# Second block's attention: probabilities turned one step later, evictions in steps of their own, bias tables issued by SyncE

## The reference, cut to what matters

```python
s = jnp.einsum('bhrnqd,bhrnkd->bhrnqk', qb, kb) * (HEAD_DIM ** -0.5)
s = s - slopes * dist            # dilated heads; masked, softmax, times v
...
s = jnp.where(mask, s + bias[None], NEG_INF)   # neighbourhood heads
p = jax.nn.softmax(s, axis=(-2, -1))
o = jnp.einsum('bhijqckl,bhijkld->bhijqcd', p, vg)
...
y_dil = rms_norm(y_dil, g_out_dil); y_na = rms_norm(y_na, g_out_na)
h = h + jnp.concatenate([y_dil, y_na], axis=-1) @ w_out
```

## Time and profile before

| | us |
|---|---|
| median of 3 runs | 2672.23 |
| lowest and highest of them | 2665.27, 2678.31 |
| the profiled execution's own time | 2675.64 |
| its span, first to last instruction | 2673.8 |
| TensorE busy over the span | 2409.8 (90%) |
| VectorE busy | 1320.0 (49%) |
| ScalarE busy | 1060.9 (40%) |
| GpSimd busy | 655.6 (25%) |

### The profile page before, as it was taken

One profiled execution on the slowest core, in us unless ns is written; L12 is line 12 of the kernel. 1 busy time (PEld: TensorE's weight loads), 2 busy tenths in 40 slices (PEclk: granted clock), 3 DMA queues, 4 the chain that ended last, 5 costly groups with the idle time before them and its releaser, 6 DMA issues.

```text
span 2673.8 us, 31894 instructions
## 1 busy us (share of the span) xinstructions
PE 2409.8 (90%) x12186; PEld 1879.8 (70%) x12186; DVE 1320.0 (49%) x2106; ACT 1060.9 (40%) x1619; POOL 655.6 (25%) x293
## 2 busy tenths in 40 slices
PE   4998977979999999979987889999989998959998
PEld 2875734858888788857564567888868765647776
DVE  3436943144341244225386215525433377539998
ACT  4324621243332233225264035434332355327776
POOL 1220000142222222232200043444454400112223
PEclk8998968979999999979998889999999988979999
DMA  6530041113322232213302232323323211229997
GB/s 229 180 103 6 1 157 48 32 32 103 111 64 64 88 107 75 63 40 117 103 6 111 79 126 72 102 87 102 102 63 110 87 49 35 95 106 341 345 350 267
DMA packets 81032, 291.17 MB, mean 109 GB/s; under 512 B 10713, under 2 KB 13050, under 8 KB 79932
## 3 DMA queue, kind: packets, MB, share of 16 engines
q1 hardware_dynamic: 71952, 251.26, 27.5%
q10 hardware_dynamic: 6348, 28.51, 3.1%
q0 software_dynamic: 2592, 9.48, 0.9%
HBM read 283.43 MB, written 9.48 MB: 110 GB/s over the span
## 4 chain that ended last, share of the span: by engine, by line
PE 75%; DVE 13%; ACT 3%; DMA 2%; issue 2%; POOL 2%; DVEq 2%; SPq 0%; ACTq 0%; POOLq 0%
PE ps L598 36%; PE ps L645 11%; PE ps L621 4%; DVE mlo L2369 4%; PE ps L1221 3%; PE ps L706 2%; DVE stat L1949 2%; PE ps L1239 2%; DVE ptl L1965 2%; PE ps L1093 2%; PE ps L1048 2%; DVE pr L1957 1%; PE ps L946 1%; POOL x L547 1%; PE ps L1066 1%
## 5 line engine op out<-in xcount | busy, mean ns | idle before, releaser
L541 POOL TENSOR_TENSOR wlo<-wraw,whi 128x1024 fp32r<-128x1024 f32 x208 | 502.3, 2416 | 1581.1 <-ACT whi L1261 936.5
L598 PE MATMUL ps<-hhi,whi 128*128 128x512 f32 x1624 | 590.3, 363 | 3.0 <-DVE hlo L2071 2.0
L598 PE MATMUL ps<-hlo,whi 128*128 128x512 f32 x1624 | 584.1, 360 | 0.0
L598 PE MATMUL ps<-hhi,wlo 128*128 128x512 f32 x1624 | 581.1, 358 | 0.0
L598 PEld LDWEIGHTS ps<-hhi,whi 128*128 128x128 f32 x1624 | 306.7, 189 | 72.3 <-issue 19.6
L598 PEld LDWEIGHTS ps<-hhi,wlo 128*128 128x128 f32 x1624 | 305.7, 188 | 47.9
L598 PEld LDWEIGHTS ps<-hlo,whi 128*128 128x128 f32 x1624 | 306.5, 189 | 45.3 <-issue 1.0
L1824 DVE SCALAR_TENSOR_TENSOR up<-ps,cconv,up 128x511 f32<-128x511 f32 (+1 forms) x132 | 83.2, 658 | 292.6 <-ACT up L1570 290.1
L2369 DVE TENSOR_TENSOR mlo<-mraw,mhi 128x1024 fp32r<-128x1024 f32 x147 | 206.5, 1434 | 6.9 <-ACT mhi L1693 6.8
L1268 ACT ACTIVATE whi<-wraw 128x1024 fp32r<-128x1024 f32 x132 | 138.9, 1052 | 149.9 <-PE ps L645 120.3
L645 PE MATMUL ps<-alo,whi 128*128 128x512 f32 (+1 forms) x528 | 188.0, 356 | 0.0
(11 more groups left out here) (337 smaller groups left out, 4248.7 us busy)
## 6 DMA issues: line engine op xcount, KB each, us to landing
wraw<-in_w_all SPq DMA_DIRECT2D x288, 512.0 KB, 3.5
mraw<-in_w_moe SPq DMA_DIRECT2D x168, 512.0 KB, 5.4
mraw_b<-in_w_mod SPq DMA_DIRECT2D x10, 512.0 KB, 15.5
fl<-in_four ACTq DMA_DIRECT2D x2, 2048.0 KB, 8.1
hd<-in_hyf ACTq DMA_DIRECT2D x2, 2048.0 KB, 8.3
hi<-in_hyi ACTq DMA_DIRECT2D x2, 2048.0 KB, 13.4
slot_rows<-in_slot_rows ACTq DMA_DIRECT2D x1, 3612.0 KB, 20.9
xs<-slot_rows POOLq DMA_DIRECT2D x7, 516.0 KB, 7.0
```

Of the source, the lines that this page charges most:

```text
L541: pool.tensor_tensor(wlo[:, slot, :], wraw[:, AT_W[n] % RING, :], whi[:, slot, :].bitcast(F32), ALU.subtract).then_inc(lo_split, 1)
L598: m = pe.matmul(ps[:, bank + b, 0:w], a, r[:, c0:c0 + w], start=k == 0 and q == 0, stop=k == KT - 1 and q == 2)
```

## The change

- The transposes of step i take the probabilities of step i-3 (T_LAG = 3) instead of i-2, and the outputs are 7 steps behind (O_LAG) instead of 6.
- ScalarE, in a step: high half of the turned probabilities of step i-3 first, then the exponential of i. The exponential's own wait for the transposes goes, since the first has it.
- The values are evicted in steps 0, 8, 16, ... by ScalarE and in steps 1, 9, ... by VectorE (before: 0, 6, 14, ... on both). TensorE still turns them in 0, 6, 14, ....
- The outputs are evicted in steps 14, 22, ..., the squares in 15, 23, ..., the outputs' low halves in 16, 24, ... (before: 13, 13, 14 and every 8 behind).
- The table's subtraction moves from q = 2 to q = 3 of the head ahead.
- The tables of heads 2 to 15 are issued by SyncE, in a loop between the ring's fetches and the wait for the last scores. The tables of heads 0 and 1 stay with ScalarE.

```diff
+    def table_half(h, a):
+        half = slice(64 * a, 64 * a + 64)
+        return half, dram["alibi"][h, half, :] if h < 8 else dram["rpbw"][h - 8, :, (1 - a) * HD:(15 - a) * HD]
+    T_LAG, O_LAG = 3, 7
...
@@ SyncE, behind the ring's fetches
+        for h in range(2, NH2):
+            sp.wait_ge(sem("min_ready"), STEPS2 + 4 * (h - 1))
+            for a in range(2):
+                half, src = table_half(h, a)
+                sp.dma_start(tab[half, h % 2, :], src).then_inc(sem("tab_in", h % 2), 16)
@@ TensorE
-        for i in range(N + 6):
+        for i in range(N + O_LAG):
...
-            if 2 <= i < N + 2:
-                pe.wait_ge(sem("p_ready"), STEPS2 + i - 1)
-                if i >= 4:
-                    pe.wait_ge(sem("pt_lo"), HALVES2 + 2 + i - 3)
+            if T_LAG <= i < N + T_LAG:
+                t = i - T_LAG
+                pe.wait_ge(sem("p_ready"), STEPS2 + t + 1)
+                if t >= 2:
+                    pe.wait_ge(sem("pt_lo"), HALVES2 + 2 + t - 1)
                 for c in range(4):
-                    m = pe.transpose(ps[:, 2 + i % 2, c * P:c * P + P], p2[:, (i - 2) % 3, c * P:c * P + P],
-                                     ident[:, :])
+                    m = pe.transpose(ps[:, 2 + t % 2, c * P:c * P + P], p2[:, t % 3, c * P:c * P + P], ident[:, :])
-            if i >= 6:
-                h, c = (i - 6) // 4, (i - 6) % 4
+            if i >= O_LAG:
+                h, c = (i - O_LAG) // 4, (i - O_LAG) % 4
@@ ScalarE
-        for i in range(N + 6):
+        for i in range(N + O_LAG + 1):
+            if T_LAG <= i < N + T_LAG:
+                t = i - T_LAG
+                h, q = t // 4, t % 4
+                act.wait_ge(sem("t_ready"), HALVES2 + t + 1)
+                if h >= 2:
+                    act.wait_ge(sem("o_ready"), UNITS2 + h - 1)
+                act.activation(pt2h[:, h % 2, :, q * P:q * P + P],
+                               ps[:, 2 + t % 2, :].rearrange("p (c n) -> p c n", c=4), ACT.Copy)\
+                   .then_inc(sem("pt_hi"), 1)
             if i < N:
                 act.wait_ge(sem("min_ready"), STEPS2 + i + 1)
-                if i >= 3:
-                    act.wait_ge(sem("t_ready"), HALVES2 + i - 2)
                 act.activation(p2[:, i % 3, :], s2[:, i % 2, :], ACT.Exp, ...
-                if i in V_STEPS:
...
+            if i % 8 == 0 and i < N:
+                v = i // 8
...
-            if i >= 13 and (i - 13) % 8 == 0:
-                tl = (i - 13) // 8
+            if i >= 14 and i % 8 == 6:
+                tl = (i - 14) // 8
...
+            if i >= 15 and i % 8 == 7:
+                tl = (i - 15) // 8
                 act.activation(out_sq(tl // 4, tl % 4), ps[:, 6 + tl % 2, :], ACT.Square).then_inc(sem("osq_ready"), 1)
-            if 1 <= i <= N:
...
-                if q == 3 and h + 2 < NH2:
-                    load_table(h + 2)
@@ VectorE
-        for i in range(4 * NH2):
+        for i in range(N + 8):
+            if i < N:
...
-            if i:
+            if 1 <= i <= N:
                 divisor(i - 1)
-            if i >= 2:
-                prob_low(i - 2)
-            if i in V_STEPS:
-                v = V_STEPS.index(i)
+            if T_LAG <= i < N + T_LAG:
+                prob_low(i - T_LAG)
+            if i % 8 == 1 and i < N:
+                v = i // 8
...
-            if i >= 14 and (i - 14) % 8 == 0:
-                output_low((i - 14) // 8)
-            if q == 2 and 8 <= h + 1 < NH2:
+            if i >= 16 and i % 8 == 0:
+                output_low((i - 16) // 8)
+            if i < N and q == 3 and 8 <= h + 1 < NH2:
                 dve.wait_ge(sem("tab_in", (h + 1) % 2), 32 * ((h + 1) // 2 + 1))
...
-        divisor(4 * NH2 - 1)
-        prob_low(4 * NH2 - 2)
-        prob_low(4 * NH2 - 1)
         output_low(KT - 1)
```

More of the change, by code:

```diff
@@ L1604, in load_table @@
         def load_table(h):
-            if h >= 2:
-                act.wait_ge(sem("min_ready"), STEPS2 + 4 * (h - 1))
             for a in range(2):
-                half = slice(64 * a, 64 * a + 64)
-                src = dram["alibi"][h, half, :] if h < 8 else dram["rpbw"][h - 8, :, (1 - a) * HD:(15 - a) * HD]
+                half, src = table_half(h, a)
                 act.dma_start(tab[half, h % 2, :], src).then_inc(sem("tab_in", h % 2), 16)
@@ L1628, in _ @@
         N = 4 * NH2
-        for i in range(N + 6):
+        for i in range(N + O_LAG + 1):
[8 more added lines that the diff above has]
+                   .then_inc(sem("pt_hi"), 1)
             if i < N:
                 act.wait_ge(sem("min_ready"), STEPS2 + i + 1)
-                if i >= 3:
-                    act.wait_ge(sem("t_ready"), HALVES2 + i - 2)
                 act.activation(p2[:, i % 3, :], s2[:, i % 2, :], ACT.Exp, bias=stat[:, i % 2, 0:1], scale=-1.0,
                                accum_out=stat[:, i % 2, 1:2]).then_inc(sem("exp_done"), 1)
-                if i in V_STEPS:
-                    v = V_STEPS.index(i)
[L1638 to L1645, removed]
-            if i >= 13 and (i - 13) % 8 == 0:
-                tl = (i - 13) // 8
+            if i % 8 == 0 and i < N:
+                v = i // 8
+                act.wait_ge(sem("vt_done"), DEPTH + v + 1)
+                if v >= 2:
+                    act.wait_ge(sem("o_ready"), UNITS2 + 2 * (v - 1))
+                for g in range(2):
+                    h = slice(64 * g, 64 * g + 64)
+                    m = act.activation(vt2h[:, v % 2, g, :, h],
+                                       ps[:, 4, :].rearrange("p (t n) -> p t n", t=4)[:, :, h], ACT.Copy)
+                m.then_inc(sem("vt2_hi"), 1)
+            if i >= 14 and i % 8 == 6:
+                tl = (i - 14) // 8
                 act.wait_ge(sem("o_ready"), UNITS2 + 2 * tl + 2)
@@ L2164, in _ @@
         dve.wait_ge(sem("tables_in"), 32)
+        N = 4 * NH2
         def prob_low(i):
@@ L2185, in output_low @@
                                      out_hi(tl).bitcast(F32), ALU.mult, ALU.subtract).then_inc(sem("attn_out"), 1)
-        for i in range(4 * NH2):
[L2188 to L2193, removed]
-            if i >= 2:
[L2195 to L2199, removed]
-            if i:
+        for i in range(N + 8):
+            if i < N:
+                h, q = i // 4, i % 4
+                tb = tab[:, h % 2, :]
+                if q == 0:
+                    dve.wait_ge(sem("tab_in", h % 2), 32 * (h // 2 + 1))
+                    dve.drain()
+                dve.wait_ge(sem("s_ready"), STEPS2 + i + 1)
+                if i >= 2:
+                    dve.wait_ge(sem("exp_done"), STEPS2 + i - 1)
+                o = (3 - q) * P
+                dve.tensor_tensor_reduce(s2[:, i % 2, :], ps[:, i % 2, :], tb[:, o:o + TX], 1.0, 3e38, ALU.add, ALU.min,
+                                         stat[:, i % 2, 0:1]).then_inc(sem("min_ready"), 1)
+            if 1 <= i <= N:
                 divisor(i - 1)
-            if i >= 2:
-                prob_low(i - 2)
-            if i in V_STEPS:
-                v = V_STEPS.index(i)
+            if T_LAG <= i < N + T_LAG:
+                prob_low(i - T_LAG)
+            if i % 8 == 1 and i < N:
+                v = i // 8
                 dve.wait_ge(sem("vt2_hi"), v + 1)
```

## The result

The changed kernel takes 2647.12 us (median of 5 runs, 2643.12 to 2654.85) against 2672.32 (5 runs): ratio 0.9905, interval 0.9878 to 0.9931. In a later session it was run again, 2652.72 us against 2674.34, ratio 0.9915 (0.9882 to 0.9947). So it is faster by 0.9%, some 25 and 22 us. The forecast was 37 us and 2635, range 2624 to 2656.

What follows compares the result with a forecast made beforehand. TensorE was taken to bound attention, with 12.65 us of holes; -10.7 holes, -15.1 clock, -12.9 start, +0.4 cross-check and +1.5 adds sum to -36.8 us, from the 2672.23 median to 2635.4, forecast 2635, range 2624 to 2656.

Steps and rivals of the forecast that it cites:

- later clock: Second block's attention behind its start: without holes over 0.5 us, 34.1 us at half clock go, -15.1 us.
- Holes: TensorE's 12.65 us of holes in attention shrink to 1.9 us left in neighbourhood periods, -10.7 us.
- the count: VectorE's lateness followed through a neighbourhood period: 18.1 us against TensorE's 18.0, leaving about 0.47 us of hole per period.
- The start: Attention's first steps: minimum 1 right behind minimum 0, scores 9 end at 2142.4 instead of 2155.3, -12.9 us.
- 1.26 brought no fall: Attention's start: full clock presumed since holes there become 0.7 and 0.5 us and holes of 1.26 brought no fall.
- the fall at the start stays: Rival for attention's start: first steps without outputs keep the clock low, 9.6 us given back, 2645 us; chance 0.22.
- the clock at half behind 2142: Sign of being wrong: granted clock in attention at half behind 2142; full clock was expected from 2131 on.
- no term of its own: Transposes a step later in attention: slack grows 2.175 us, which only makes the other parts pay; no separate gain.
- SyncE's tables 0: Table DMAs moved from ScalarE to SyncE: ScalarE loses 14 pairs of 1.12 us but isn't the bound; 0 by itself.
- GpSimd's adds +1.5: GpSimd's adds of squares meet VectorE's products in the loop and hold them: 0 to 4.4 us, taken as +1.5.
- Tail 0: From the end of scores 63 to the last output: 9.2 us before, 9.05 after, counted as 0.
- taken 0.4 off: Cross-check from scores 9 to 63: 27.3 us left beside holes and later clock; 0.4 us taken off the gain.

Runs made afterwards that it cites:

- the filled kernel of before: Kernel before with 8 unread 128x496 matmuls ahead of the transposes of steps 32, 40, 48 and 56; 2659.23 us, ratio 0.9954.
- table by GpSimd: Changed kernel with the subtraction of the neighbourhood tables moved from VectorE to GpSimd, between its adds of squares; 2660.88 us, ratio 0.9962.
- the second trace: Trace of the unaltered changed kernel run once more in a later session; 2652.72 us, ratio 0.9915; stage 164.2 us, 34.1 us at half clock.
- a version with smaller holes: Kernel before with only the tables of heads 2 to 15 issued by SyncE; 2675.08 us, ratio 1.0011; stage 195.0 us.
- a later run: Changed kernel with values evicted in steps 3, 11, ... and their low halves in 4, 12, ...; 2646.92 us, ratio 0.9899.

## Why the prediction was right, and where it was not

**Direction, mechanism, later clock: right.** The step that all hung on, that holes over 2 us bring the later falls, is shown by the filled kernel of before; the term was 15.1 us and 34.1 us of low clock went to 0. Its size is that of one execution; by the medians of that run it is nearer 10. Nor are 2 us a bound: holes of 1.33 to 1.47 us brought falls too (table by GpSimd).

**Holes: -10.7 forecast, -9.6 measured** (12.65 to 3.08). The place and the waiter were right, the size 0.88 instead of 0.47. What the count had too small is the table's subtraction: from its start to the next minimum 1.27 us pass (2200.33 - 2199.06), not 1.00, since VectorE stands 0.18 us behind it. That makes 0.74 of the 0.88; 0.14 stay open. VectorE's eight steps are so 18.6 us and not 18.1 (seven from 2197.21 to 2214.00 and one of 1.84), against TensorE's 17.8: level it was not, but the bound.

**The start: -12.9 forecast; this is the term that failed.** The end of scores 9, which the forecast reckons with, came 29.62 us behind the start of scores 0 before, 23.50 after: -6.1 in the profiled pair, and at the second trace's 25.27, -4.3. The order of work was right: VectorE took minimum 1 behind minimum 0 and scores 4 started 6.07 us behind scores 0 (forecast 6.1). What failed is the sentence that presumed full clock because "1.26 brought no fall". A hole's length alone does not decide: single holes of 1.25 us inside the heads brought no fall, and at the stage's entry one came in every unfilled trace, in seven of ten before the hole ahead of scores 2 was over, with the hole of 0.78 us ahead of scores 0 as the only finished one before it. The prediction counted the holes ahead of scores 2 and 4, and left that one out. The low clock in the profiled execution cost 17.1 x 0.442 = 7.5 us by the estimate; the start fell short by 6.8. The rival "the fall at the start stays" (2645) is what happened, and the median is 2 us from it. Its reason, no outputs in those steps, is not borne out: with the holes filled the clock was low for 6.8 us, and with work in place of the outputs as well for 6.8 again. The prediction named the clock at half behind 2142 as a sign of being wrong; it was low until 2146.1.

**Lag "no term of its own":** right within 1.3 us. **SyncE's tables 0:** right for the changed kernel; on the kernel before alone no change. **GpSimd's adds +1.5:** one product held 0.51 us, and behind it the hole of 0.44 us (counted in the 3.08); the term was too large. No minimum waited for a table: they landed 3.0 to 3.8 us behind their issue. **Tail 0:** from the last scores' end to the last outputs 9.2 us before, 8.8 after.

**Sum for the profiled pair:** holes 9.6, later clock 15.1, start 6.1 and tail 0.4 make 31.2 where the stage gained 30.3. From the end of scores 9 to the start of scores 63 it gained 23.8 us (148.35 to 124.51) and not 9.6 + 15.1 = 24.7; the prediction had met this and taken 0.4 off. The other 7 of the 37 are the start. The medians show less than the trace, 25, because the changed kernel's profiled execution was the fastest of its five and that of before was 3.4 us above its median.

What stays open: why the clock's low stretch at the start lasts 17.1 us in one execution of the changed kernel and 34.1 in another, why it begins 2.3 us behind scores 0 in one and 5.4 in another, and whether the hole ahead of scores 0 alone, filled, would keep the clock up.

## What to carry to other kernels

Spread what comes once in a while over steps that each have spare time on every engine it touches, and follow the lateness through the period: here that, with the DMA issues moved, brought by estimate 11 of 12 us of pace, an added step of lag 1.3. Then price a hole in TensorE by the clock behind it, not by its length: 12.65 us of holes had 15 us of loss by slow clock with them in one execution, and a version with smaller holes ran slower in its trace. Where engines wait at a stage's entry, unread matmuls in the gap can pay (2642.23 against 2652.72 us in one session), as long as they do not set the pace.

## What was not expected of the hardware

- The granted clock fell at a stage's entry behind a hole of 0.78 us, in seven of ten unfilled traces before the next one (0.74) was over and in three behind both, and not in the two with all holes filled; holes of 1.25 us inside the dilated heads brought none in two kernels, two each.
- Holes of 1.33 to 1.47 us in the neighbourhood heads brought a fall three times of three, for 10.2, 10.2 and 17.1 us.
- The low stretch behind the same start lasted 17.1 us in one execution and 34.1 in another of the same kernel.
- GpSimd's subtraction of 128x896 took 2.09 us and held a VectorE product of 0.49 us, which took 1.72.
- An add of squares and a VectorE product recorded as starting 0.02 us before it met in the tail of a later run: the product took 1.59 us instead of 0.49, the add 1.28.
